# First expert loads and the router's matrix issued beside the output projection, norm and routing in one stage, the first block's rows picked by one-hot products

## The chip, the cores and the metric

The kernel runs on one core of a Trainium2 chip. Its time is the device time of one execution in microseconds (us), and the number compared is the median of several executions. All arithmetic is in 32-bit floating point.

## The reference, cut to what matters

The program is a chain of transformer layers over 512 tokens of width 1024. The last two layers (0 and 1 here) each end in a mixture of experts. The part that the change touches:

```python
h = _rms(x, norm2_w[layer]) * (1 + scale2) + shift2
x = x + gate2 * _hier_moe(h, ...)

def _hier_moe(h, ...):              # 512 tokens, 4 groups of 8 experts
    g_logits = xt @ w_group + b_group
    g_sel = argmax(g_logits)
    e_in = (xt @ w_expert + b_expert)[group g_sel]
    top_v, top_i = lax.top_k(e_in, 2)
    gate = softmax(g_logits)[g_sel] * softmax(top_v)
    # tokens are grouped by expert in blocks of rows; for each block:
    #   (silu(xr @ w1[e]) * (xr @ w3[e])) @ w2[e]
    # and each token's two results are summed with its gates
```

Each expert has 1024x512 matrices w1 and w3 and a 512x1024 matrix w2, so the 32 experts of a layer hold 192 MB (in units of 1024 x 1024 bytes).

## The kernel before

One SBUF tensor (`arena`) is cut into regions by hand, and the eight PSUM banks are used by number. The program is a row of `nc.Block()` stages. In a stage each engine has its own list of instructions, written out by hand with semaphore waits, and all engines meet at a barrier where a stage ends. For each of the two layers the end of the work looks like this:

1. `project_out` (L1742): the mixer's output projection, 64 products, the residual, and the sum of squares for the next norm. The sync engine (SP, which issues the big loads) has only the last two dense weight tiles to issue here (L235).
2. `apply` (L405): a stage of its own. The vector engine (DVE) multiplies x by the reciprocal norm in eight parts (L396), the scalar engine (ACT) adds gain and shift to each (L403) and so makes `h`. SP clears 58 semaphores (layer 0) of stages that have ended.
3. `experts` (L2727), which begins with the routing (`route`, L2486):
   - SP issues the router's matrix `wr` (L2545) and then ten expert loads of 1 MB (L2786), into a ring of 14 slots. A later load n waits until load n-14 has been used.
   - TensorE (PE) multiplies router and `h` (L2551), folds the halves (L2555) and turns `h` into rows of tokens (L2561). ACT copies these rows to SBUF (L2596) and stores them in a DRAM tensor `token_rows` (L2601).
   - DVE picks the experts (L2623 to L2636). PE ranks each token within its expert (L2567, L2568) and counts (L2570). DVE makes one-hot matrices `A` of the ranks for the experts 0 and 1 (L2645), PE makes the token lists of these two experts from them (L2575), and GpSimd (POOL) fetches the rows of the first two blocks from `token_rows` by an indirect DMA (L2833).
   - DVE goes on with the order of the experts by count (to L2661), which SP waits for, and with the place of every token (to L2721). PE lays the places out (`place_tensor`, L2582 and L2587) between block 0 and block 1.
4. The 15 blocks of experts (`KINDS`): a block holds the rows of one ("w"), two ("p") or four ("q") experts. The blocks 0 and 1 (`FIXED`) are always the experts 0 and 1. For block i PE turns the rows of block i+1 (`turn`, L2849), does the first layer in four quarters (`hidden`, L2866), turns the result (L2876), does the second layer (`output`, L2890) and adds the block before into the tokens by a one-hot product (`scattered`, L2904).

Between the blocks 1 and 2 SP waits for more than its ring:

```python
if i == FIXED:
    sp.wait_ge(self.order_ready, 1)
    for n in range(FIXED):
        sp.wait_ge(x_in[n], x_in_before[n] + 16)
```

Before it reads the order it so waits until both early gathers have landed; after that it reads four expert numbers and issues load 10.

Of the kernel before, what the change touches and what calls it, by code (L numbers as in the profile page):

```python
# [45 lines left out]
MOE_SLOT = 2048  # L46
NEG = -30000.0
# [99 lines left out]
class Program:  # L147
    def __init__(self, nc, ins, out):
# [6 lines left out]
        self.output_stored = nc.alloc_semaphore("output_stored")  # L155
        total = 0
# [247 lines left out]

    def apply(self, name, job):  # L405

        nc = self.nc
        scaled, ready = self.sem(name + "_scaled"), self.sem(name + "_ready")
        with nc.Block() as block:
            @block.sync  # L410
            def _(sp):
                self.clear_past(sp)

            @block.vector
            def _(dve):
                self.scale_steps(dve, [job], scaled)

            @block.scalar
            def _(act):
                self.shift_steps(act, [job], scaled, ready)  # L420
        self.release_past()
# [1320 lines left out]
    def project_out(self, name, w0, src, gate, gain, scale, norms=None):  # L1742
# [137 lines left out]
    def even_mixer(self):  # L1880
# [23 lines left out]
        self.project_out("even_out", TILE0["even_out"], o, self.mod["even"][:, 16:24],  # L1904
# [452 lines left out]
    def odd_mixer(self):  # L2357
# [17 lines left out]
        self.project_out("odd_out", TILE0["odd_out"], o, self.mod["odd"][:, 16:24],  # L2375
# [110 lines left out]
    def route(self, layer):  # L2486
# [5 lines left out]
        wr = self.view(self.r0, KD, HALF)  # L2492
# [20 lines left out]
        early_rank, early_own = new(4 * FIXED, 1), new(FIXED, 4)  # L2513
# [17 lines left out]
        s = {n: self.sem("route_" + n) for n in ["w", "lg", "turned", "kept", "stored", "e", "ex", "oh", "rank", "ab", "tok",  # L2531
# [7 lines left out]
        logits, ranks, counts = small[:, 0:144], small[:, 160:288], small[:, 288:320]  # L2539
# [4 lines left out]
        def sync_steps(sp):  # L2544
            sp.dma_start(wr, self.ins["w_route"][layer].rearrange("p (k m) -> p k m", k=KD)).then_inc(s["w"], 16)  # L2545

        def tensor_steps(pe):
            pe.wait_ge(s["w"], 16)
            for k in range(KD):
                part = slice(HALF * (k % 2), HALF * (k % 2) + HALF)  # L2550
                mm = pe.matmul(self.bank[4][part, :], wr[:, k, :], h[:, k, :], start=(k < 2), stop=(k >= KD - 2))  # L2551
# [13 lines left out]
            for b in range(4):  # L2565
                for a in range(b):
# [40 lines left out]
        def vector_steps(dve):  # L2607
            def do(ins):
                self.dve.after(dve, ins)
# [714 lines left out]
```

## Time and profile before

| what | value |
|---|---|
| time, median of 3 runs | 3175.17 us (3168.21 to 3175.97) |
| profiled execution, its own time | 3168.01 us |
| profiled execution, its span | 3166.1 us |
| PE busy | 2819.5 us, 89% of the span |
| DVE busy | 1482.2 us, 47% |
| ACT busy | 644.5 us, 20% |
| data moved by DMA | 615.87 MB |

A share of busy time says how much an engine did, not whether it was waited for. What a change in one place is worth is read from the chain of releases at that place: what an engine waited for, and who ended that wait. The routing of layer 0 stands at about 1682 to 1750 us of the span and the one of layer 1 at about 2583 to 2652 us; both have the same instructions.

### The profile page before, as it was taken

What the parts mean: (1) busy time and instruction counts of PE and PEld (TensorE: products, weight loads), DVE (VectorE), ACT (ScalarE), POOL (GpSimd) and SP (SyncE); (2) the same over time, 40 slices, a digit from 0 to 9 for tenths busy, and PEclk for the clock granted to TensorE, in tenths of its full rate; (3) what the DMA queues carried; (4) which work ended last, traced back from release to release, by engine and by line L of the source; (5) the groups of instructions that cost most, each with busy time, mean ns of one, the idle gap of its engine ahead of it and who ended that gap; (6) DMA issues with size and microseconds to landing.
All of it is one profiled execution on the core that took longest, in us unless ns stands there. A gap on an engine that the chain in (4) does not pass through costs nothing. (4 is left out here: it accounts for less than half of the span.)

```text
span 3166.1 us, 36578 instructions
## 1 busy us (share of the span) xinstructions
PE 2819.5 (89%) x13980; PEld 1796.4 (57%) x13980; DVE 1482.2 (47%) x2937; ACT 644.5 (20%) x1350; POOL 159.7 (5%) x171
## 2 busy tenths in 40 slices
PE   6989779999989998989896989789799878998897
PEld 4877557788838887858653433233387534332242
DVE  4567465657635675456434223132544623232234
ACT  3111455445521110011232000000103421000000
POOL 0000021222100000000100000000000000000000
PEclk8899989999999999999797999899899988999899
DMA  6111147663022222221005999998322028999996
GB/s 242 54 40 61 59 168 258 241 230 118 28 80 80 87 86 73 87 68 67 27 14 228 375 420 385 418 419 342 145 90 71 7 117 336 419 419 383 420 367 250
DMA packets 112200, 615.87 MB, mean 195 GB/s; under 512 B 12864, under 2 KB 13328, under 8 KB 62096
## 3 DMA queue, kind: packets, MB, share of 16 engines
q1 hardware_dynamic: 101456, 576.67, 47.0%
q0 software_dynamic: 9408, 32.54, 2.9%
q10 hardware_dynamic: 1152, 4.19, 0.3%
q8 instruction: 117, 1.92, 0.2%
q14 instruction: 67, 0.55, 0.1%
HBM read 604.84 MB, written 8.51 MB: 194 GB/s over the span
## 5 line engine op out<-in xcount | busy, mean ns | idle before, releaser
L2866 PE MATMUL bank<-arena 128*32 128x512 f32 (+2 forms) x2048 | 440.6, 618 | 35.6 <-DMA arena<-in_w 33.2
L453 PE MATMUL bank<-arena 128*128 128x256 f32 x1776 | 412.1, 386 | 31.5 <-DVE arena L506 11.9
L453 PEld LDWEIGHTS bank<-arena 128*128 128x128 f32 x1776 | 340.6, 193 | 99.1 <-issue 35.6
L2866 PEld LDWEIGHTS bank<-arena 128*32 128x32 f32 (+2 forms) x2048 | 151.4, 137 | 297.1 <-issue 293.9
L2890 PE MATMUL bank<-arena 128*32 128x512 f32 (+2 forms) x1024 | 239.1, 700 | 52.8 <-DMA arena<-in_w 52.8
L2904 PE MATMUL bank<-arena 128*128 128x512 f32 x480 | 237.3, 619 | 8.4 <-DVE arena L3031 4.9
L248 PE MATMUL bank<-arena 128*128 128x512 f32 (+1 forms) x608 | 218.1, 518 | 14.8 <-DVE arena L665 13.9
L2996 DVE SCALAR_TENSOR_TENSOR arena<-bank,arena 128x512 f32<-128x512 f32 x240 | 180.1, 751 | 55.2 <-PE bank L2904 42.5
L2890 PEld LDWEIGHTS bank<-arena 128*32 128x32 f32 (+2 forms) x1024 | 80.2, 148 | 209.0 <-issue 209.0
L248 PEld LDWEIGHTS bank<-arena 128*128 128x128 f32 x608 | 119.7, 198 | 110.4 <-issue 101.5
L2904 PEld LDWEIGHTS bank<-arena 128*128 128x128 f32 x480 | 75.1, 188 | 168.6 <-DVE arena L2996 125.7
L2982 DVE COPY arena<-bank 128x512 f32<-128x512 f32 x30 | 20.8, 692 | 251.4 <-PE bank L2890 251.4
L3006 DVE TENSOR_TENSOR arena<-arena,bank 128x512 f32<-128x512 f32 x30 | 20.6, 688 | 221.4 <-ACT arena L2955 221.4
L1488 PE MATMUL bank<-arena 128*128 128x256 f32 x528 | 118.8, 380 | 0.0
L1124 ACT ACTIVATE arena<-bank 128x256 f32<-128x256 f32 x288 | 93.6, 383 | 87.3 <-PE bank L1044 64.9
L1488 PEld LDWEIGHTS bank<-arena 128*128 128x128 f32 x528 | 100.5, 190 | 14.9
L2935 ACT ACTIVATE arena<-bank 128x512 f32<-128x512 f32 x30 | 18.0, 598 | 438.3 <-PE bank L2849 438.3
L1044 PE MATMUL bank<-arena 128*128 128x128 f32 x576 | 98.7, 294 | 1.5 <-DVE arena L1239 0.8
L1044 PEld LDWEIGHTS bank<-arena 128*128 128x128 f32 x576 | 75.9, 192 | 39.6 <-issue 31.2
L1236 DVE TENSOR_TENSOR arena<-bank,arena 128x256 f32<-128x256 f32 x144 | 61.0, 423 | 75.9 <-PE bank L1029 75.8
L1029 PE MATMUL bank<-arena 128*128 128x128 f32 x576 | 94.3, 286 | 0.6
L2971 DVE COPY arena<-bank 128x512 f32<-128x512 f32 x26 | 18.0, 692 | 159.4 <-PE bank L2849 159.4
(451 smaller groups left out, 4111.0 us busy)
## 6 DMA issues: line engine op xcount, KB each, us to landing
arena<-in_w SPq DMA_DIRECT2D x384, 1024.0 KB, 20.6
arena<-in_dense SPq DMA_DIRECT2D x308, 512.0 KB, 4.5
arena<-core_rows POOLq DMA_DIRECT2D x48, 256.0 KB, 6.4
arena<-in_xT SPq DMA_DIRECT2D x2, 2048.0 KB, 12.6
token_rows<-arena ACTq DMA_DIRECT2D x8, 512.0 KB, 12.6
gdn_gate<-arena POOLq DMA_DIRECT2D x8, 256.0 KB, 2.7
arena<-gdn_gate SPq DMA_DIRECT2D x1, 2048.0 KB, 8.4
arena<-band_bias POOLq DMA_DIRECT2D x2, 1024.0 KB, 6.1
```

The lines of the kernel that those rows point to most:

```text
L248: mm = eng.matmul(dst, w[:, k, :], src[:, k, :], start=(k == 0), stop=(k == KD - 1))
L453: mm = pe.matmul(out, w[:, k, :], x[:, k, :], start=(k == 0), stop=(k == K1 - 1))
L1029: mm = pe.matmul(Y[u][:, q, :], buf[u]["bl"][:, q, :], buf[u]["xl"][:, u, q, :], start=True, stop=True)
L1044: mm = pe.matmul(touched(X[u][:, 2 * q:2 * q + 2, :], l, u), buf[u]["zs"][:, q, :], buf[u]["yn"][:, q, :], start=False, stop=(l == 6), ski ...
L1124: act.activation(gathered(buf[u]["xl"][:, side, :, :], l + 1), touched(X[u], l + 1, side), ACT.Copy).then_inc(kept, 1)
L1236: dve.tensor_tensor(buf[u]["yn"], Y[u][:, 0:2, :], levels[:, l - 1, :, :].to_broadcast([P, 2, P]), ALU.mult).then_inc(s["yn"], 1)
L1488: mm = pe.matmul(product(m, p), s4[:, t, k, :], ht[:, t, k, :], start=(k == 0), stop=(k == K1 - 1))
L2866: mm = pe.matmul(self.bank[2 + t][part, :], xT[i % 2][:, 2 * q + k, part], w[j][:, k, t, :], start=(q == 0 and k == 0), stop=(q == 3 and k ...
L2890: mm = pe.matmul(self.bank[7 - t][part, :], aT[:, 2 * q + k, part], w[j][:, k, 512 * t:512 * t + 512], start=(q == 0 and k == 0), stop=(q ...
L2904: pe.matmul(self.bank[4 + k % 2][:, :], y[i % 2][:, k * P:(k + 1) * P], scatter[i % 2], start=True, stop=True).then_inc(s["summed"], 1)
L2982: dve.tensor_copy(y[i % 2][:, 512:1024], self.bank[6][:, :]).then_inc(s["yk0"], 1)
L2996: dve.scalar_tensor_tensor(self.x[:, k, :], self.bank[4 + k % 2][:, :], gate[:, k:k + 1], self.x[:, k, :], ALU.mult, ALU.add).then_inc(s[" ...
```

## The change

- SP issues the router's matrix and the first 6 (layer 0) or 10 (layer 1) expert loads at the end of its list in `project_out`, into slots that are free by then (`MOE_ORDER`, `MOE_EARLY`).
- The stage `apply` is gone; its steps stand at the head of `experts`, and the router's product k waits for part k of `h` alone.
- The ranks take four products in place of ten, and DVE is released before the counts.
- The rows of block 0 are no longer gathered from DRAM and turned: 32 products of `rows` (tokens x width) with the one-hot `A` of expert 0 write them, turned, into the banks 0 and 1. Only block 1 is gathered.
- `A` now holds the token's own mask too (rank + 1, compared with iota + 1), and is made in one instruction for each expert.
- The token list of expert 1 is made by PE behind the 32 products.
- SP waits for the order alone before load 10. SP's clearing of semaphores stands at the head of `experts`.

```diff
+MOE_ORDER = [[8, 9, 10, 11, 12, 2, 7, 0, 1, 3, 4, 5, 6, 13], list(range(MOE_RING))]
+MOE_EARLY = [6, 10]
...
+    def early_experts(self, sp, layer):
+
+
+        sp.dma_start(self.router(), self.ins["w_route"][layer].rearrange("p (k m) -> p k m", k=KD)).then_inc(self.router_loaded, 16)
+        for n in range(MOE_EARLY[layer]):
+            if n < 4 * FIXED:
+                src = self.ins["w13"][layer, n // 4, :, n % 4 * MOE_SLOT:(n % 4 + 1) * MOE_SLOT]
+            else:
+                src = self.ins["w2"][layer, 0, :, (n - 4 * FIXED) * MOE_SLOT:(n - 4 * FIXED + 1) * MOE_SLOT]
+            sp.dma_start(self.expert_slot(layer, n), src).then_inc(self.expert_loaded[n], 16)
...
             def _(sp):
                 self.load_until(sp, w0 + KD, ahead=0)
+                self.early_experts(sp, layer)
...
         def tensor_steps(pe):
-            pe.wait_ge(s["w"], 16)
+            pe.wait_ge(self.router_loaded, 16 * (layer + 1))
             for k in range(KD):
+                pe.wait_ge(ready, k + 1)
...
             pe.wait_ge(s["oh"], 1)
-            for b in range(4):
-                for a in range(b):
-                    pe.matmul(ranks[:, b * 32:b * 32 + 32], self.C("ones"), oh12[:, a, :], start=(a == 0), stop=False)
-                pe.matmul(ranks[:, b * 32:b * 32 + 32], self.C("stri"), oh12[:, b, :], start=(b == 0), stop=True)
+            pe.matmul(ranks, self.C("stri"), oh12, start=True, stop=False, skip_group_check=True)
+            for a in range(3):
+                mm = pe.matmul(ranks[:, 32 * a + 32:P], self.C("ones"), oh12[:, a:a + 1, :].to_broadcast([P, 3 - a, 32]),
+                               start=False, stop=(a == 2), skip_group_check=True)
+            mm.then_inc(s["rank"], 1)
+            pe.wait_ge(s["kept"], 8)
             for b in range(4):
                 mm = pe.matmul(counts, self.C("ones"), oh12[:, b, :], start=(b == 0), stop=(b == 3))
             mm.then_inc(s["rank"], 1)
             pe.wait_ge(s["early"], 1)
-            for j in range(FIXED):
+            for k in range(KD):
                 for b in range(4):
-                    mm = pe.matmul(early_toks[:, j:j + 1], A[:, 4 * j + b, :], early_own[:, j, b:b + 1],
+                    mm = pe.matmul(self.bank[k // 4][:, k % 4 * P:(k % 4 + 1) * P], rows[:, b, k * P:(k + 1) * P], A[:, b, :],
+                                   start=(b == 0), stop=(b == 3))
+            mm.then_inc(first_turned, 1)
+            pe.wait_ge(s["early"], FIXED)
+            for j in range(1, FIXED):
+                for b in range(4):
+                    mm = pe.matmul(early_toks[:, j:j + 1], A[:, 4 * j + b, :], self.C("tok")[:, b:b + 1],
                                    start=(b == 0), stop=(b == 3))
             mm.then_inc(s["early_made"], 1)
...
-            dve.tensor_copy(early_rank.rearrange("p (e b) o -> p e (b o)", b=4), rk[:, :, 0:FIXED].rearrange("p b e -> p e b"))
-            do(dve.tensor_tensor(early_own, oh12[:, :, 0:FIXED].rearrange("p b e -> p e b"),
-                                 tok.to_broadcast([P, FIXED, 4]), ALU.mult))
-            dve.tensor_tensor(A[:, 0:4 * FIXED, :], c3("iota", 4 * FIXED), wide(early_rank, P), ALU.is_equal
-                              ).then_inc(s["early"], 1)
+
+            do(dve.scalar_tensor_tensor(early_rank.rearrange("p (e b) o -> p e (b o)", b=4), rk[:, :, 0:FIXED].rearrange("p b e -> p e b"),
+                                        1.0, oh12[:, :, 0:FIXED].rearrange("p b e -> p e b"), ALU.add, ALU.mult))
+            for j in range(FIXED):
+                mine = slice(4 * j, 4 * j + 4)
+                dve.scalar_tensor_tensor(A[:, mine, :], c3("iota", 4), 1.0, wide(early_rank[:, mine, :], P), ALU.add, ALU.is_equal
+                                         ).then_inc(s["early"], 1)
+            dve.wait_ge(s["rank"], 2)
             do(dve.tensor_copy(cn, c2))
...
             dve.wait_ge(s["early_made"], 1)
-            dve.tensor_copy(self.early_tok, early_toks).then_inc(s["early_tok"], 1)
+            dve.tensor_copy(self.early_tok[:, 1:FIXED], early_toks[:, 1:FIXED]).then_inc(s["early_tok"], 1)
...
-                route_sync(sp)
+                self.clear_past(sp)
                 for i in range(N + 1):
                     if i == FIXED:
                         sp.wait_ge(self.order_ready, 1)
-                        for n in range(FIXED):
-                            sp.wait_ge(x_in[n], x_in_before[n] + 16)
...
                 pool.wait_ge(self.rows_stored, 64)
                 pool.wait_ge(self.early_ready, 1)
-                for i in range(N):
+                for i in range(1, N):
...
                 route_tensor(pe)
-                turn(0)
...
+                self.shift_steps(act, [job], scaled, ready)
                 route_scalar(act)
                 keep(0)
+                act.wait_ge(self.rows_stored, 64)
...
+                self.scale_steps(dve, [job], scaled)
                 route_vector(dve)
...
-        p.apply(name + "2", (h, p.x, L, p.norm_r[0], p.mod["g1"], mod[:, 24:32]))
-        p.experts(layer, mod[:, 40:48])
+        p.experts(layer, (h, p.x, L, p.norm_r[0], p.mod["g1"], mod[:, 24:32]), mod[:, 40:48])
```

The first place is TensorE's list in layer 0 from the router's product to the first half of block 0. Before, with the ranks at L2567 and L2568, the counts at L2570, the token lists at L2575 and the turn of block 0 at L2849:

```order
L2551 MATMUL bank<-arena 64x512 x8
L2555 MATMUL bank<-arena 128x36 x4
L2561 MATMUL bank<-arena 128x128 x32
L2568 MATMUL bank<-arena 128x32
L2567 MATMUL bank<-arena 128x32
L2568 MATMUL bank<-arena 128x32
L2567 MATMUL bank<-arena 128x32 x2
L2568 MATMUL bank<-arena 128x32
L2567 MATMUL bank<-arena 128x32 x3
L2568 MATMUL bank<-arena 128x32
L2570 MATMUL bank<-arena 128x32 x4
L2575 MATMUL bank<-arena 128x1 x8
```

Behind these stand the 8 turns of L2849 and `hidden`. After, in the same place (L2571 and L2573 are the ranks, L2578 the counts, L2583 the one-hot products, L2589 the token list of expert 1, L2884 is `hidden`):

```order
L2557 MATMUL bank<-arena 64x512 x8
L2561 MATMUL bank<-arena 128x36 x4
L2567 MATMUL bank<-arena 128x128 x32
L2571 MATMUL bank<-arena 128x128
L2573 MATMUL bank<-arena 128x96
L2573 MATMUL bank<-arena 128x64
L2573 MATMUL bank<-arena 128x32
L2578 MATMUL bank<-arena 128x32 x4
L2583 MATMUL bank<-arena 128x128 x32
L2589 MATMUL bank<-arena 128x1 x4
L2884 MATMUL bank<-arena 128x512 x8
```

Ten rank products became four wider ones, and 32 products of 128 columns stand between the counts and the token list, whose own 8 products became 4; the 8 turns behind them are gone.

The second place is SP's list in layer 0, from the last two dense tiles to the wait for the order. L221 is the clearing of semaphores, TENSOR_LOAD the reading of an expert's number. Before:

```order
L235 DMA arena<-in_dense 128x1024 x2
L1746 UNCONDITIONAL_BRANCH
L410 UNCONDITIONAL_BRANCH
L221 ISA x58
L409 UNCONDITIONAL_BRANCH
L2781 UNCONDITIONAL_BRANCH
L2545 DMA arena<-in_w_route 128x512
L2786 DMA arena<-in_w 128x2048 x10
L2799 TENSOR_LOAD arena
```

After:

```order
L240 DMA arena<-in_dense 128x1024 x2
L1740 DMA arena<-in_w_route 128x512
L1746 DMA arena<-in_w 128x2048 x6
L1752 UNCONDITIONAL_BRANCH
L2799 UNCONDITIONAL_BRANCH
L226 ISA x58
L2806 DMA arena<-in_w 128x2048 x4
L2819 TENSOR_LOAD arena
```

The router's matrix and six of the ten loads moved ahead of the stage's end; one barrier (two branches) is gone, and the 58 clears stand ahead of the last four loads.

The third place is DVE's list around the token lists. Before, the wait for PE's token lists is in front of the CAST at L2657:

```order
L2642 COPY arena<-bank 128x8
L2643 TENSOR_TENSOR arena<-arena 128x8
L2645 TENSOR_TENSOR arena<-arena 128x1024
L2647 COPY arena<-bank 128x32
L2653 TENSOR_TENSOR arena<-arena 128x32
L2654 TENSOR_TENSOR arena<-arena 128x1024
L2655 TENSOR_REDUCE arena<-arena 128x32
L2657 CAST arena<-bank 128x2
L2658 TENSOR_TENSOR arena<-arena 128x1024
```

After, with the same wait in front of the CAST at L2673:

```order
L2656 SCALAR_TENSOR_TENSOR arena<-bank,arena 128x8
L2660 SCALAR_TENSOR_TENSOR arena<-arena 128x512 x2
L2663 COPY arena<-bank 128x32
L2669 TENSOR_TENSOR arena<-arena 128x32
L2670 TENSOR_TENSOR arena<-arena 128x1024
L2671 TENSOR_REDUCE arena<-arena 128x32
L2673 CAST arena<-bank 128x1
L2674 TENSOR_TENSOR arena<-arena 128x1024
```

The one-hot matrices come in two instructions of half the size; the place of the CAST in the list is the same, but what it waits for on PE now stands behind the 32 products.

## Rows read from the trace of the kernel before

**Rows 1.** The page: span and TensorE's busy time.
```profile
span 3166.1 us, 36578 instructions
...
PE 2819.5 (89%) x13980; PEld 1796.4 (57%) x13980; DVE 1482.2 (47%) x2937; ACT 644.5 (20%) x1350; POOL 159.7 (5%) x171
```

**Rows 2.** The chain that ended last, layer 1's routing: start, duration, what ran.
```profile
2589.48 2.95 DMA arena<-in_w_route
2592.47 5.45 PE bank L2551 x16
...
2605.77 15.99 DMA token_rows<-arena
...
2629.60 9.11 PE bank L2866 x16
...
2646.46 1.70 PE bank L2582 x16
```

**Rows 3.** Timeline, layer 0: start, duration, engine, line, [idle before, releaser].
```profile
1682.70 5.75 ACT L403 ACTIVATE arena<-arena 128x512 f32<-128x512 f32 x8 [1.02 <-DVE arena L396]
...
1691.48 5.36 PE L2551 MATMUL bank<-arena 128*64 128x512 f32 x16 [11.19 <-DMA arena<-in_w_route]
```

**Rows 4.** Timeline, layer 0: from the ranks to the token lists.
```profile
1705.56 0.41 PE L2568 MATMUL bank<-arena 128*128 128x32 f32 x2 [1.63 <-DVE arena L2635]
...
1707.81 1.18 PE L2570 MATMUL bank<-arena 128*128 128x32 f32 x8
...
1709.31 1.23 DVE L2645 TENSOR_TENSOR arena<-arena 128x1024 f32<-128x1024 f32 x1
...
1710.59 3.57 PE L2575 MATMUL bank<-arena 128*128 128x1 f32 x16 [1.59 <-DVE arena L2645]
```

**Rows 5.** Timeline, layer 0, PE from block 0's turn to the places.
```profile
1725.51 1.97 PE L2849 MATMUL bank<-arena 128*128 128x128 f32 x8 [11.35 <-DMA arena<-token_rows,arena]
1728.70 9.00 PE L2866 MATMUL bank<-arena 128*128 128x512 f32 x16 [1.22 <-ACT arena L2935]
...
1745.30 1.86 PE L2582 MATMUL bank<-arena 128*128 128x31 f32 x16
1747.00 3.82 PE L2587 MATMUL bank<-arena 128*128 128x128 f32 x32
```

**Rows 6.** Timeline, layer 0, DVE: token lists kept, order, last place step; a 128x512 SCALAR_TENSOR_TENSOR.
```profile
1714.27 0.16 DVE L2657 CAST arena<-bank 128x2 uint32<-128x2 f32 x1 [0.90 <-PE bank L2575]
...
1718.11 0.18 DVE L2661 CAST arena<-arena 128x32 int32<-128x32 f32 x1
...
1732.46 0.28 DVE L2721 TENSOR_TENSOR arena<-arena 128x124 f32<-128x124 f32 x1
...
1773.42 0.74 DVE L3027 SCALAR_TENSOR_TENSOR arena<-arena 128x512 f32<-128x512 f32 x1
```

**Rows 7.** SP, layer 0: issues up to 1727, its wait, issues from 1726 on.
```profile
L2786 SPq DMA_DIRECT2D arena<-in_w x10: 424/442/486, 1689.1 to 1693.5; - x10
...
SPq L2806 <- DMA arena<-token_rows,arena: 33.6, 1, 33.6
...
1730.22 27.98 SPq L2786 DMA_DIRECT2D arena<-in_w  x10
```

**Rows 8.** Times to landing: stores of L2601, then gathers of L2833 (min/median/max).
```profile
DMA to landing us min/median/max: 8.1/12.6/16.0
...
DMA to landing us min/median/max: 4.3/8.5/9.7
```

**Rows 9.** Windows: busy time by engine, granted TensorE clock, DMA share, GB/s.
```profile
1705.00:1709.00 4.00, 3.44 (x28) 3.30 (x28) 0.54 (x3) 0.42 (x2) 0.00 (x0) 0.95 1.00 411
1710.00:1714.00 4.00, 3.41 (x16) 3.41 (x16) 3.27 (x5) 0.00 (x0) 0.00 (x0) 0.50 1.00 419
```

**Rows 10.** Waits in layer 0 (1680 to 2240): PE for expert weights.
```profile
PE bank L2890 <- DMA arena<-in_w: 27.7, 9, 6.3
...
PE bank L2866 <- DMA arena<-in_w: 18.4, 5, 7.6
```

More of the change, by code:

```diff
@@ L155, in __init__ @@
         self.output_stored = nc.alloc_semaphore("output_stored")
+        self.expert_loaded = [nc.alloc_semaphore(f"expert_loaded{i}") for i in range(MOE_RING)]
+        self.router_loaded = nc.alloc_semaphore("router_loaded")
         total = 0
@@ L1740, in project_all, with expert_slot, router, project_out @@
         self.release_past()
-    def project_out(self, name, w0, src, gate, gain, scale, norms=None):
+    def expert_slot(self, layer, n):
+        at = self.free0 + 8192 + MOE_SLOT * MOE_ORDER[layer][n % MOE_RING]
+        return self.cols(at, MOE_SLOT)
+    def router(self):
+        return self.view(self.free0 + 4096, KD, HALF)
+    def early_experts(self, sp, layer):
[6 more added lines that the diff above has]
+            sp.dma_start(self.expert_slot(layer, n), src).then_inc(self.expert_loaded[n], 16)
+    def project_out(self, name, layer, w0, src, gate, gain, scale, norms=None):
         nc = self.nc
@@ L2538, in route @@
         small = self.bank[5]
-        logits, ranks, counts = small[:, 0:144], small[:, 160:288], small[:, 288:320]
+        logits, ranks, counts = small[:, 0:144], small[:, 160:288], self.bank[6][:, 0:32]
         toks, early_toks = small[:, 320:320 + BLOCKS], self.bank[4][:, 0:FIXED]
@@ L2723, in vector_steps, with experts @@
             dve.tensor_copy(self.slot_tok, toks).then_inc(s["slots"], 1)
-        return sync_steps, tensor_steps, place_steps, scalar_steps, vector_steps
-    def experts(self, layer, gate):
+        return tensor_steps, place_steps, scalar_steps, vector_steps
+    def experts(self, layer, job, gate):
         nc = self.nc
-        route_sync, route_tensor, place_tensor, route_scalar, route_vector = self.route(layer)
+        route_tensor, place_tensor, route_scalar, route_vector = self.route(layer)
+        scaled, ready = self.sem("moe_norm_scaled"), self.sem("moe_norm_ready")
         f = self.free0
-        ring = self.view(f + 8192, MOE_RING, MOE_SLOT)
         assert f + 8192 + MOE_RING * MOE_SLOT <= self.total - 128
@@ L2765, in experts @@
                                                "yk0", "yk1", "spread", "scatter", "summed", "added"]}
-        loaded = [self.sem(f"moe_slot_loaded{i}") for i in range(MOE_RING)]
+        loads = 6 * NE
+        loaded_before = [layer * ((loads - r + MOE_RING - 1) // MOE_RING) for r in range(MOE_RING)]
         x_in = [self.software_sem(f"moe_rows_gathered{i}") for i in range(2)]
-        x_in_before = [16 * layer * evens, 16 * layer * odds]
-        nth = lambda i: 16 * (i // 2 + 1)
+        x_in_before = [16 * layer * (evens - 1), 16 * layer * odds]
+        nth = lambda i: 16 * ((i + 1) // 2)
         spare_sync, spare_gpsimd, spare_tensor, spare_scalar, spare_vector = self.spare_blocks(layer, gate)
@@ L2776, in slot_in @@
         def slot_in(eng, n):
-            eng.wait_ge(loaded[n % MOE_RING], 16 * (n // MOE_RING + 1))
-            return ring[:, n % MOE_RING, :]
+            r = n % MOE_RING
+            eng.wait_ge(self.expert_loaded[r], 16 * (loaded_before[r] + n // MOE_RING + 1))
+            return self.expert_slot(layer, n)
         with nc.Block() as block:
```

34 lines of the change are left out of this document (11 added, 23 removed).

## The prediction

> **What bounds the kernel now.** I read the page first: TensorE is busy 89% of a span of 3166.1 us [rows 1], but that is an average, and the change touches only two places, the start of the experts in layer 0 and in layer 1. So I read the chain that ended last there. In layer 1 it goes from the load of the router's matrix (2589.48) over the router's product, the turning and ACT's copies to the store of the token rows, which takes 15.99 us to land, then over the gather to the first expert product at 2629.60 and the placing at 2646.46 [rows 2]. TensorE does almost nothing useful for some 37 us of that. Layer 0 is the same story: router's product at 1691.48, placing at 1745.30, a distance of 53.82 us against 53.99 in layer 1 [rows 2, 3, 5]. I therefore work out layer 0 and double it.
>
> After the first blocks PE is in turns bound by itself and by the weights: in layer 0 it waits 27.7 and 18.4 us for weights in 14 waits [rows 10]. So a gain at the front has to be checked against the weight stream too.
>
> **Part 1, apply and experts in one stage.** Before, ACT's last shift ends at 1682.70 + 5.75 = 1688.45. The barrier, the issue and the landing of the router's matrix follow, and the 16 passes of the product, 5.36 us, which end at 1696.84 [rows 3]. After, the matrix is there, and product k follows part k of `h`. ACT's pace is 5.75/8 = 0.72 us a part and PE's mean 5.36/8 = 0.67, so PE keeps up, and one product with its tail is left behind the last part, 1.0 us: end at 1689.4, gain 7.4 us. Bounds: 0.5 us behind (gain 7.9), and PE starting one part late and lagging 2 us behind (gain 6.4). The 58 clears move to SP's list in this stage; behind them stand only loads 6 to 9, which block 1 and block 0's second layer use some 30 us later, and in layer 1 no load: cost nothing. The early loads start when SP's last dense tile is issued; SP has nothing else there, and the output projection has its weights ahead of them in the same queue: nothing as well.
>
> **Part 2, ranks and one-hot.** From the start of the ranks at 1705.56 to the start of the token lists at 1710.59 are 5.03 us [rows 4]. After: four rank products are 8 passes, at the 1.18 us that the 8 passes of L2570 take; one small DVE step and its hand-over, 0.3; a 128x512 SCALAR_TENSOR_TENSOR, 0.74 [rows 6]; hand-over 0.1. Sum 2.3 us, gain 2.7 (bounds 2.2 and 3.0). PE's counts, another 1.18, end at about the same time. DVE's part up to here is not changed. So the one-hot products can start at 1710.59 - 7.4 - 2.7 = 1700.5.
>
> **Part 3, the 32 products.** They are new. Each is two passes, 64 in all. The nearest row is L2587, 32 passes of 128x128 in 3.82 us, 0.12 us each [rows 5]: 7.5 us at the high clock. At 1.2 GHz they would be twice that, 15 us. The granted clock was 0.95 of full while the ranks ran and 0.50 while the token lists ran, behind a short idle time [rows 9]. After the change PE has less idle time ahead of this point, so I take the high clock for most of it, 8.5 us: end at 1709.0. Bounds 7.3 and 15. The Trainium skill (page "TensorE: Matmul & The Clock Gate", "The HAM clock gate") says that the lower clock is the default and that activity has to release it; by that alone the products would begin slow, and this is a rival below. The trace agrees that clock and activity go together here: 0.50 at 1710 after the gap.
>
> Then PE makes expert 1's token list, 8 passes. Before, 16 passes took 3.57 us at the low clock [rows 4], so 0.9 to 1.8; I take 0.9: E = 1709.9. Block 0 needs ACT's copies, 1.2 us behind the products (L2866 was idle 1.22 for them [rows 5]), so `hidden(0)` begins at about 1710.2, where it was 1728.70. That is 18.5 us.
>
> **Part 4, what is late next.** The gain is not all kept. DVE waits at the CAST (L2657) for PE's token list, and that now stands behind the 32 products. From this CAST at 1714.27 to the last place step at 1732.46 + 0.28 are 18.5 us of DVE work [rows 6] that the change leaves alone. Before it was long done when PE reached the placing at 1745.30. After, it ends at E + 18.5 = 1728.4. PE arrives there two half blocks and a turn after `hidden(0)` began: 16.6 us before (1728.70 to 1745.30, the first part at the low clock), so 1726.8 at the latest, and with a warm clock about 1725. It waits 1.6 to 3.4 us. So the placing starts at 1728.4 instead of 1745.30: **gain 16.9 us per layer**, set by DVE and not by the gather.
>
> Other waits in this stretch: block 1's gather is issued at E + 0.5 and lands 4.3 to 9.7 us later [rows 8], needed about 8 us behind E; if it is late by 2 us, the wait at the placing swallows it. The stores of the token rows took up to 16.0 us [rows 8] behind ten queued loads; now at most four loads are ahead, and PE's products give them 10 us more. ACT's new wait for them stands behind `keep(0)`: nothing.
>
> **Part 5, the weight stream.** Before, SP issued ten loads up to 1693.5, idled 33.6 us for the gathers and issued load 10 at 1730.22, some 3 us after its wait [rows 7]. After, it waits for the order alone: that is 4.0 us after the CAST (1718.29 - 1714.27 [rows 6]), plus 3 us of reading: E + 7 = 1716.9. That is 13.3 us earlier than before, 3.6 less than the gain of PE. A load is 1.05 MB at 419 GB/s [rows 9], 2.5 us. Loads 10 to 17 take 20 us, to about 1737.5, and load 18 may start when block 1's first quarter is used, at 1728.4 + 5.4 (places) + 3.4 = 1737.2. From there PE frees a slot every 3.4 us in a one-expert block, so the stream has caught up before the first weight wait. Cost nothing, if this holds.
>
> **Sum.** Two layers by 16.9, and 0.2 for layer 1's longer stretch: 34 us. The profiled execution took 3168.01 us by its own time, 0.2% below the median; it would be 3134. On the median, 3175.17 - 34 = **3141 us**.
>
> **Rivals.**
> *The clock.* The 32 products run at 1.2 GHz to the end: 6.5 us more per layer, all of it in DVE's wait too. Gain 2 x 10.4 = 21: 3154. For it: 0.50 behind the gap [rows 9]. Against it: the products are dense, and the 16 passes of the router's product were not slow to the end.
> *The weight stream decides.* If PE is held by the weights from load 10 on, the gain is that of load 10, 13.3 per layer: 27, 3149. For it: 46 us of weight waits per layer [rows 10]. Against it: ring and one-expert blocks give time to catch up.
> *DVE is no limit.* If PE gets to the placing later than DVE or the products take only 7.3 us and E comes early, the gain is up to 18.5 to 20 per layer: 3136.
> *The other side, block 1's gather behind the weight stream.* Its rows have nothing ahead before; now the loads 10 to 17 are let go 6 us behind it. It decides when it lands over 27 us after its issue, since need (8), slack at the placing (2) and the gain (17) are then used up. If all 14 slots' loads went ahead of its packets, 14 x 2.5 + 4.3 = 39 us, it would cost 12 us more per layer than is won: 3199. Against it: 9.7 us is the longest gather in a trace full of loads [rows 8]. The Trainium skill (page "DMA: Bandwidth & Descriptors", "Issuing engines are not separate DMA queues") says that transfers of all engines share the same 16 DMA engines and interleave, so a gather has no lane of its own. The trace agrees for the stores, 16.0 us with ten loads in flight.
>
> **How the numbers follow.** My forecast (gain of 30 to 38) 0.66, weight stream 0.12, the clock 0.12, DVE no limit 0.06, gather 0.02, and 0.02 that the early gain is lost elsewhere so that nothing is left. Before's own runs lie within 3168 to 3176, so a change under 0.3%, 9.5 us, can't be told from none. The range takes in the clock rival and the gain of 20 per layer with a run at the low end: 3127 to 3156. Faster 0.95, same 0.02, slower 0.03.
>
> **What the profile would show.** Router's product ending about 1 us behind the last shift; the products' start about 12 us behind that shift, and 8 to 9 us for 64 passes; `hidden(0)` 18 us earlier; a new wait of PE for DVE of 1.6 to 3.4 us in front of the placing; load 10 about 7 us behind the CAST; weight waits in sum as before. I am wrong if the products run at the low clock, if weight waits grow by what was won, or if PE waits for the gather in front of block 1's turn.

## The result, and the profile after

The changed kernel takes 3149.72 us (median of 4 runs, 3144.84 to 3150.47), the kernel before, run beside it, 3175.57 us (4 runs, 3168.21 to 3177.84). The ratio is 0.9926, with a 95% interval of 0.9913 to 0.9939: 19 to 28 us faster. The forecast was 3141 us, a gain of 34. So the sign and the place are right, and about 8 of the 34 us are missing.

The page of the changed kernel (its profiled run took 3149.28 us), against [rows 1]:

```profile
span 3147.5 us, 36685 instructions
...
PE 2838.1 (90%) x14052; PEld 1818.0 (58%) x14052; DVE 1483.0 (47%) x2937; ACT 644.1 (20%) x1350; POOL 158.2 (5%) x169
```

The span is 18.6 us shorter, and TensorE is busy 18.6 us longer. Its 72 additional instructions account for part of that; the other part are old products that take longer, as the timeline shows.

Because one trace reaches layer 0's routing a few us earlier or later than another (1680 to 1685 us in the traces of this study), I count from an anchor: DVE's first step of the norm's scaling, at 1681.97 in the trace of before and at 1684.23 in that of after. A "+" in the text is a time from there, in layer 0 unless it says otherwise. Timeline of TensorE after the change: start, duration, engine, line, [idle before, releaser].

```profile
1685.92 6.15 PE L2557 MATMUL bank<-arena 128*64 128x512 f32 x16 [3.37 <-ACT arena L408]
...
1700.79 0.80 PE L2571 MATMUL bank<-arena 128*128 128x128 f32 x2 [1.64 <-DVE arena L2649]
1701.38 1.33 PE L2573 MATMUL bank<-arena 128*128 128x96 f32 x6
1702.52 1.90 PE L2578 MATMUL bank<-arena 128*128 128x32 f32 x8
1704.22 8.91 PE L2583 MATMUL bank<-arena 128*128 128x128 f32 x64
1712.97 0.95 PE L2589 MATMUL bank<-arena 128*128 128x1 f32 x8
1714.36 7.12 PE L2884 MATMUL bank<-arena 128*128 128x512 f32 x16 [0.43 <-issue]
1721.32 1.03 PE L2867 MATMUL bank<-arena 128*128 128x128 f32 x8
1722.19 7.05 PE L2884 MATMUL bank<-arena 128*128 128x512 f32 x16
1732.60 3.59 PE L2596 MATMUL bank<-arena 128*128 128x31 f32 x16 [3.37 <-DVE arena L2737]
1736.01 6.46 PE L2601 MATMUL bank<-arena 128*128 128x128 f32 x32
1742.31 7.05 PE L2884 MATMUL bank<-arena 128*128 128x512 f32 x16
```

The first experts' product (L2884, L2866 before) starts at +30.13 instead of +46.73. The placing (L2596 and L2601, before L2582 and L2587 of [rows 5]) starts at +48.37 instead of +63.33, behind a wait of 3.37 us for DVE. But it then takes 9.71 us to the start of block 1's product, where it took 5.35 us before. So block 1 starts at +58.08 instead of +68.68: of 16.6 us at block 0, 15.0 are left at the placing and 10.6 behind it. Layer 1 does the same: idle 3.37 us, L2596 3.59, L2601 6.56, block 1's product at +58.58. The distance between the two layers' anchors shrank by 10.5 us (900.77 to 890.26), which says that what is gained at block 1 arrives whole at the next layer.

The windows of the changed kernel over this stretch say why the placing got slower: busy time of each engine, then the granted TensorE clock as a share of full, DMA share, GB/s.

```profile
1726.00:1730.00 4.00, 3.23 (x8) 1.14 (x6) 3.59 (x14) 0.60 (x1) 0.00 (x0) 1.00 1.01 426
1730.00:1734.00 4.00, 1.40 (x7) 1.43 (x7) 2.35 (x5) 0.00 (x0) 0.00 (x0) 0.67 1.01 424
1734.00:1738.00 4.00, 4.00 (x20) 4.00 (x20) 0.79 (x2) 0.00 (x0) 1.00 (x2) 0.50 1.02 418
1738.00:1742.00 4.00, 4.00 (x23) 4.00 (x22) 0.00 (x0) 1.68 (x3) 0.92 (x1) 0.55 1.00 413
1742.00:1746.00 4.00, 4.00 (x14) 2.02 (x13) 0.00 (x0) 0.71 (x2) 0.00 (x0) 1.00 0.70 281
```

The clock was at 1.00 until the wait, fell in it, and stayed at about half (1.2 GHz; the windows give 0.50 and 0.55) for the whole placing. DVE's list shows whom PE waited for, against [rows 6]:

```profile
1714.03 0.16 DVE L2673 CAST arena<-bank 128x1 uint32<-128x1 f32 x1 [6.65 <-PE bank L2589]
1717.87 0.18 DVE L2677 CAST arena<-arena 128x32 int32<-128x32 f32 x1
...
1732.18 0.28 DVE L2737 TENSOR_TENSOR arena<-arena 128x124 f32<-128x124 f32 x1
```

DVE stands still for 6.65 us in front of a 0.16 us CAST, because the token list that it copies is now made behind the 32 one-hot products.

### The profile page after: what moved, and what is told of

Read it like the earlier page. It is cut to its first block and busy times, and to the rows that moved or that the text cites. A ratio compares the mean times of both kernels' runs of the same rounds, so it can differ in the third digit from the quotient of the medians.

```text
span 3147.5 us, 36685 instructions
## 1 busy us (share of the span) xinstructions
PE 2838.1 (90%) x14052; PEld 1818.0 (58%) x14052; DVE 1483.0 (47%) x2937; ACT 644.1 (20%) x1350; POOL 158.2 (5%) x169
## 5 line engine op out<-in xcount | busy, mean ns | idle before, releaser
L2884 PE MATMUL bank<-arena 128*32 128x512 f32 (+2 forms) x2048 | 437.2, 619 | 30.9 <-DMA arena<-in_w 30.1
L2884 PEld LDWEIGHTS bank<-arena 128*32 128x32 f32 (+2 forms) x2048 | 149.9, 137 | 289.6 <-issue 288.6
```

The source lines that it names most:

```text
L2884: mm = pe.matmul(self.bank[2 + t][part, :], xT[i % 2][:, 2 * q + k, part], w[j][:, k, t, :], start=(q == 0 and k == 0), stop=(q == 3 and k ...
```

## The experiments

The theory after the result: DVE's 6.65 us make PE wait 3.37 us at the placing, and that wait costs twice, as idle time and as 4.4 us of placing at the low clock. The rivals: the gather of block 1 or the weight stream limits what is won; the one-hot products are a bad exchange whoever waits; the early loads carry the gain, or none of it. Nine of the ten kernels below change one or two things in the changed kernel or put parts of it back, and one repeats it. Ratios are against the kernel before, with the 95% interval.

**1. The CAST later.** DVE's wait for the token list and its CAST stand 5.9 us of DVE's own work later, behind the order (L2677) and eight small steps, where it still waits 0.70 us for the list and no longer 6.65:

```diff
-            dve.wait_ge(s["early_made"], 1)
-            dve.tensor_copy(self.early_tok[:, 1:FIXED], early_toks[:, 1:FIXED]).then_inc(s["early_tok"], 1)
...
             x1, x2 = (x.rearrange("p a b -> p (a b)") for x in (m1, m2))
+            dve.wait_ge(s["early_made"], 1)
+            dve.tensor_copy(self.early_tok[:, 1:FIXED], early_toks[:, 1:FIXED]).then_inc(s["early_tok"], 1)
```

> DVE keeps the token list of expert 1 (the CAST of L2673) 5.9 us of its own work later, just behind the ranks of both choices (L2688), and so no longer stands still while PE makes the 32 one-hot products. Theory A (what was lost of the forecast is PE's wait for DVE in front of the placing, 3.37 us, and the low clock that follows it, which stretches the 16 + 32 passes of the placing from 5.35 to 9.71 us): DVE's last place step ends some 5.9 us earlier, PE does not wait, the placing takes about 5.4 us, block 1 starts 7.7 us earlier in each layer: 15 us less than the changed kernel, about 3135. Theory B (the weight stream decides from load 10 on): PE starts block 1 earlier but waits that much more for weights; within 3 us of the changed kernel.

Measured: 3138.85 us, ratio 0.9902 (0.9887 to 0.9918). Better than the change, but not the 3135 that was expected. The timeline of this kernel:

```profile
1711.09 7.12 PE L2885 MATMUL bank<-arena 128*128 128x512 f32 x16 [0.43 <-issue]
1721.17 1.95 PE L2868 MATMUL bank<-arena 128*128 128x128 f32 x8 [2.96 <-DMA arena<-token_rows,arena]
1722.91 7.91 PE L2885 MATMUL bank<-arena 128*128 128x512 f32 x16
1730.66 1.86 PE L2596 MATMUL bank<-arena 128*128 128x31 f32 x16
1732.37 3.82 PE L2601 MATMUL bank<-arena 128*128 128x128 f32 x32
1736.02 7.05 PE L2885 MATMUL bank<-arena 128*128 128x512 f32 x16
```

The wait for DVE is gone and the placing is as fast as before, 1.86 and 3.82 us. In its place PE now waits 2.96 us for block 1's gather, one piece earlier, and pays behind that wait too (a turn of 1.95 instead of 1.03, a half block of 7.91 instead of 7.05). Block 1's product starts at +55.05. In layer 1 it is the same: a wait of 2.73 us, and +55.06. SP's timeline of this kernel from 1706 to 1730, and then the gather's own line, with its start and its time to landing:

```profile
1710.73 17.15 SPq L2807 DMA_DIRECT2D arena<-in_w  x7
```

```profile
L2852 POOL DMA_INDIRECT arena<-token_rows,arena x1: 1035/1035/1035, 1711.8 to 1711.8; - x1
...
DMA to landing us min/median/max: 9.4/9.4/9.4
```

The order is ready sooner, so SP issues load 10 at 1710.73, 1.1 us ahead of the gather. The gather takes 9.4 us. In the changed kernel SP issues load 10 at 1720.69, 5.7 us behind the gather, whose line reads:

```profile
L2851 POOL DMA_INDIRECT arena<-token_rows,arena x1: 1194/1194/1194, 1715.0 to 1715.0; - x1
...
DMA to landing us min/median/max: 4.6/4.6/4.6
```

It lands in 4.6 us, half the time. In layer 1 the two times are 9.2 and 4.8 us.

**2. The wait filled.** The changed kernel with PE kept busy where it waits for DVE. The four products write to a bank that nobody reads:

```diff
                         pe.wait_ge(s["kept0"], 2)
+                        for _ in range(4):
+                            pe.matmul(self.bank[7][:, :], self.C("ones"), self.x[:, 0, :], start=True, stop=True)
                         place_tensor(pe)
```

> The changed kernel with four more products of 128x512 (8 passes, about 3.4 us) on PE in front of the placing, whose result nothing reads: PE works where it waited for DVE. The moment at which DVE is ready is not moved. Theory A says that the 4.4 us by which the placing became longer come from the clock that falls in the wait: with PE busy the placing takes about 5.4 us instead of 9.7 and the kernel is 8 to 9 us faster than the changed one, though it does more work. Rival: the placing is slower for another reason (DMA traffic beside it, what it reads), then it stays at 9.7 us and the time is the same or a little above.

Measured: 3136.38 us, ratio 0.9894 (0.9879 to 0.9909). The timeline of this kernel, and behind it one of its windows:

```profile
1722.24 7.05 PE L2884 MATMUL bank<-arena 128*128 128x512 f32 x16
1729.13 3.60 PE L2936 MATMUL bank<-arena 128*128 128x512 f32 x8
1732.56 1.95 PE L2596 MATMUL bank<-arena 128*128 128x31 f32 x16
1734.34 3.82 PE L2601 MATMUL bank<-arena 128*128 128x128 f32 x32
1737.99 7.05 PE L2884 MATMUL bank<-arena 128*128 128x512 f32 x16
```

```profile
1734.00:1738.00 4.00, 4.00 (x38) 4.00 (x38) 0.79 (x2) 1.79 (x3) 1.91 (x2) 1.00 1.02 424
```

DVE's last place step ends where it did (+48.20), and so the placing starts where it did (+48.28), but PE is busy until then, and the placing takes 5.4 us instead of 9.7; the clock is 1.00. Block 1's product is at +53.71, 4.37 us before the changed kernel (4.42 in layer 1). DVE, and the DMA traffic beside the placing (424 GB/s against 418), are as before. Four products without any use make the kernel 0.3% faster, some 11 us where 8 to 9 were expected. That the clock is a cost of its own, apart from the wait, is shown by this.

**3. No one-hot products.** Both first blocks are gathered and turned as before; one stage, early loads, four rank products remain.

```diff
-            for k in range(KD):
-                for b in range(4):
-                    mm = pe.matmul(self.bank[k // 4][:, k % 4 * P:(k % 4 + 1) * P], rows[:, b, k * P:(k + 1) * P], A[:, b, :],
-                                   start=(b == 0), stop=(b == 3))
...
-            for j in range(1, FIXED):
+            for j in range(FIXED):
...
                 route_tensor(pe)
+                turn(0)
```

> One part undone: the rows of block 0 are gathered from DRAM and turned as before, both token lists are made as in one step, the 32 one-hot products are gone; the early loads, the merged stage and the four rank products stay. Theory A': the one-hot products stand in DVE's way, and what they replace had become cheap once no weight loads are queued ahead of the stores (they land in 2.8 to 3.9 us). Then: token lists done about 7 us earlier, gather lands about 5 us behind, hidden of block 0 starts within 2 us of the changed kernel, DVE is ready before PE, the placing is warm: block 1 starts 5 us earlier per layer, about 3140, faster than the changed kernel by 10. Rival (the products are what brought the gain, the gather is slow): hidden of block 0 starts 8 us or more later, 3160 or more.

Measured: 3142.6 us, ratio 0.9914 (0.99 to 0.9927), and its timeline:

```profile
1701.22 3.57 PE L2583 MATMUL bank<-arena 128*128 128x1 f32 x16
1710.33 1.97 PE L2861 MATMUL bank<-arena 128*128 128x128 f32 x8 [5.53 <-DMA arena<-token_rows,arena]
1713.52 9.35 PE L2878 MATMUL bank<-arena 128*128 128x512 f32 x16 [1.22 <-ACT arena L2947]
```

Block 0 starts at +32.34, only 2.2 us behind the changed kernel. Its first half takes 9.35 us instead of 7.12, but PE never waits for DVE, and block 1's product is at +54.64 (+55.06 in layer 1): 3.4 us *before* the changed kernel, where 5 were expected. So in the change as built the one-hot products, its most laborious part, lose 3.4 us per layer. In the medians this is inside the intervals, so it rests on the timelines of both layers.

**4. The same with the gap filled.** `no_onehot`, and four such products without use behind the token lists, where PE waits 5.53 us for the gather:

```diff
                 route_tensor(pe)
+                for _ in range(4):
+                    pe.matmul(self.bank[7][:, :], self.C("ones"), self.x[:, 0, :], start=True, stop=True)
                 turn(0)
```

> This is the version without the one-hot products (both first blocks are gathered and turned, no_onehot), with four 128x512 products by ones into a free bank put behind the token lists, where TensorE was idle for 5.53 us until the gather of block 0 had landed. It asks how much of what the one-hot products can give (block 1's products at +50.2 in late_cast_wait against +54.64 in no_onehot, from the norm's first step) is earlier rows, and how much is that TensorE comes warm to block 0. Warmth theory: the turn takes 1.03 us instead of 1.97 and the first half block 7.1 instead of 9.35, all at the same gather time (turn at about +29.2), so block 1 begins at +51.5, 3.1 us per layer before no_onehot, and the time is about 3136. Rival, the rows' time alone counts: the turn and the half block stay at 1.97 and 9.35 us although the gap is filled, block 1 stays at +54.6 and the time at about 3143. If the four products take more than the gap, because they begin at the low clock, up to 1.7 us of the gain is lost.

Measured: 3138.39 us (3131.02 to 3144.62), ratio 0.9892 (0.9869 to 0.9914), timeline:

```profile
1705.50 5.22 PE L2921 MATMUL bank<-arena 128*128 128x512 f32 x8
1711.16 1.09 PE L2861 MATMUL bank<-arena 128*128 128x128 f32 x8 [0.45 <-DMA arena<-token_rows,arena]
1713.48 7.12 PE L2878 MATMUL bank<-arena 128*128 128x512 f32 x16 [1.22 <-ACT arena L2949]
```

The rows land at the same time (the turn starts at +29.16 against +29.15), but the turn takes 1.09 instead of 1.97 us and the half block 7.12 instead of 9.35. Block 1's product is at +51.55 (+52.64 in layer 1, where the gather landed later and the turn starts at +30.25). The granted clock is 1.00 at 1709 to 1713, where it was 0.50 in `no_onehot`. So a TensorE that comes to block 0 at the full clock is a large part of what the one-hot products can give: of the 4.5 (layer 0) and 4.6 us (layer 1) by which `late_cast_wait` (9 below) starts block 1 ahead of `no_onehot`, the filled gap gives 3.1 and 2.4. The intervals of `no_onehot` and this kernel overlap, so this too rests on the timelines.

**5. The early expert loads taken away.** `MOE_EARLY = [0, 0]`; the router's matrix is still early.

> One part undone: no expert load is issued beside the output projection, all ten stand behind the 58 clears in the merged stage; the router's matrix is still early. Theory: block 0 needs its first four loads 26 us behind the stage's start, they take 10, so they are not late; the stores of the token rows have up to ten loads ahead and take up to 16 us again, so that the gather of block 1 is issued about 2 us later and lands at the limit of its need; what that costs is hidden in the wait in front of the placing. Same as the changed kernel within 3 us. Rival: the early loads are what brought the gain; then 8 us or more slower than the changed kernel.

Measured: 3143.33 us, ratio 0.9917 (0.9903 to 0.9931). Not slower than the change. The stores of the token rows landed late again. The view lists the eight stores of both layers, but has times to landing only for the four of layer 1:

```profile
L2615 ACTq DMA_DIRECT2D token_rows<-arena x8: 325/326/353, 1692.0 to 2583.8; - x8
...
DMA to landing us min/median/max: 9.9/13.2/16.5
```

In the changed kernel the same view gives 2.8/3.8/3.9, again for layer 1 alone. For layer 0 there is a wait instead: here POOL waits for the stores until 1712.79, 16.3 us behind the issue of the last one, and in the changed kernel it does not wait for them at all. But block 0 needs no stored rows now, and block 1 has DVE's wait to cover its late gather: PE waits 1.41 us for the gather and then only 1.71 us for DVE, where it was 3.37 us in one piece. Block 1's product is at +55.44 in layer 0 and +58.36 in layer 1, where PE waits 3.35 us for DVE in one piece again.

**6. Only the early issues.** The norm's stage is put back, the one-hot products taken out. What remains: early loads and router's matrix, four rank products, SP's shorter wait.

```diff
+        p.apply(name + "2", (h, p.x, L, p.norm_r[0], p.mod["g1"], mod[:, 24:32]))
...
-                self.shift_steps(act, [job], scaled, ready)
                 route_scalar(act)
...
-                self.scale_steps(dve, [job], scaled)
                 route_vector(dve)
```

> What is left of the change when the one-hot products are undone and the norm's apply is again a stage of its own: the early loads and router's matrix, the four rank products, the short wait of SP. By the profile before: the router's product starts 2.5 us earlier (no load to wait for), ranks and lists take 3.5 us less, the stores of the token rows no longer take 16 us, the gather lands behind the token lists in 5 us. Block 1 starts at about 59 us instead of 68.7: 9.5 us per layer, 19 in all, 3154 against a median before of 3173. If early loads are worth nothing by themselves (the kernel without them was as fast as the changed one) because something else hides them, it is worth 6 us or less in all.

Measured: 3151.88 us, ratio 0.9938 (0.9924 to 0.9951). The router's product starts at +6.78 (before +9.51), the ranks at +20.50 (+23.59), block 0's turn at +32.62 (+43.54), block 1's product at +58.09 and, in layer 1, +58.69. This gives 10.6 us in layer 0 at the same point where the whole change gives 10.6. The largest piece is the stores: their time to landing is 2.6/4.0/5.9 us (least, median, most; 5.3 to 5.9 in layer 0, where four loads are still issued 8 us ahead of them, 2.6 to 2.7 in layer 1, where none is) and not 8.1/12.6/16.0 [rows 8]. In layer 0 the first gather so waits for the token list alone and goes out at +27.86 instead of +38.98.

**7. The change again**, beside the same runs of before as the kernels 6, 8 and 9.

> The changed kernel once more, unchanged, as the measure for the others on the same chip. Its ratio to the kernel before should be 0.992 to 0.993 again; block 1 starts 58.1 us behind the first vector step of the norm's apply, in both layers within 0.5.

Measured: 3147.88 us (3142.33 to 3151.4), ratio 0.9924 (0.9911 to 0.9938). Block 1 starts at +58.11 in layer 0 and at +58.73 in layer 1, a little outside the 0.5 us.

**8. SP's wait for the gather put back**, alone:

```diff
                         sp.wait_ge(self.order_ready, 1)
+                        sp.wait_ge(x_in[1], x_in_before[1] + 16)
```

> The changed kernel with SP's wait for block 1's gather put back in front of load 10, nothing else. The gather is issued 1 us behind the CAST and lands 4.6 us later, some 2 us behind the order's end, so load 10 goes out about 1.5 to 2 us later. Theory: the stream catches up before its first wait, and the time is that of the changed kernel within 2 us. Rival (the weight stream decides): 3 to 4 us more.

Measured: 3146.14 us, ratio 0.9917 (0.9904 to 0.9931), block 1's product at +58.06, though load 10 goes out 1.5 us later (+38.00 against +36.46): no difference that can be told from the change.

**9. Both: the CAST later and SP's wait.** The two diffs of 1 and 8 together, so that nothing is issued ahead of the gather.

> The late CAST, and SP waits again for block 1's gather before load 10. With the late CAST alone the gather took 9.4 us (4.6 in the changed kernel), since loads 10 to 13 were let go 1 us ahead of it, and PE waited 2.7 to 3.0 us for it with the clock falling. Theory A (DVE's wait and the clock set the changed kernel's loss; the gather then takes over): gather lands in 4.6 us, PE waits for nothing between block 0 and the placing, block 1 starts 50.3 us behind the first vector step instead of 55.1 (late CAST alone) and 58.1 (changed): 15 us less than the changed kernel, 9 less than the late CAST alone. Theory B (weight stream): load 10 now goes out 7 us later than with the late CAST alone, PE pays it back in weight waits and the time is that of the late CAST alone.

Measured: 3128.41 us (3124.22 to 3129.4), ratio 0.9861 (0.9846 to 0.9876). This is the fastest version, 44 us faster than before and 19 us faster than the change in the same comparison. Its timeline:

```profile
1713.38 7.12 PE L2886 MATMUL bank<-arena 128*128 128x512 f32 x16 [0.43 <-issue]
1720.34 1.03 PE L2869 MATMUL bank<-arena 128*128 128x128 f32 x8
1721.21 7.05 PE L2886 MATMUL bank<-arena 128*128 128x512 f32 x16
1728.10 1.86 PE L2596 MATMUL bank<-arena 128*128 128x31 f32 x16
1729.80 3.82 PE L2601 MATMUL bank<-arena 128*128 128x128 f32 x32
1733.45 7.04 PE L2886 MATMUL bank<-arena 128*128 128x512 f32 x16
```

From block 0 to block 1 PE waits for nobody, and every piece has its fast duration. Block 1's product is at +50.19 (+50.47 in layer 1), 18.5 us before that of the old kernel. Load 10 goes out at +38.01, 8.2 us later than in `late_cast`, and yet PE's waits for expert weights in layer 0 are 25.3 and 16.8 us, not more than before.

**10. The fastest version without early expert loads.**

> This is the fastest version so far (late_cast_wait: DVE's wait for the token list behind the order, SP waits for block 1's gather) with the router's matrix and the expert loads not issued early, MOE_EARLY = [0, 0] (the matrix itself stays early). In the change as built the early expert loads were worth nothing, since the token rows are not needed by block 0 and DVE's wait covered the rest. Theory: here no wait covers them. The token rows land 13 to 16.5 us after their issue instead of 3.8, so block 1's gather is issued some 1 to 2 us later than in late_cast_wait and takes 6.6 us as in no_early; TensorE waits about 1.4 us for it in layer 0 and more in layer 1, so block 1 begins at +51.6 or later instead of +50.2, and the time is 3131 to 3135. Rival: the early loads are worth nothing here either, block 1 at +50.2 and a time of 3128.

Measured: 3133.57 us, ratio 0.9875 (0.9859 to 0.9892). In layer 0 PE waits 0.79 us for the gather and block 1's product is at +51.83; in layer 1 there is no wait (+50.63). The expectation had a longer wait in layer 1, and that did not come. By the timelines the early loads are worth 1.6 and 0.2 us here at most: 0.6 of the 1.6 is already there at block 0's start (+30.75 against +30.12), where the changed kernel's own two traces give +30.13 to +30.64. The medians differ by 5 us, with overlapping intervals.

## Why the prediction was right and where it was wrong

*Part 1* (one stage) said that the router's product ends 1.0 us behind the last shift, gain 7.4 us. It ends 1.36 us behind it (1685.92 + 6.15 against ACT's last shift, which ends at +6.48), and the gain is 7.0 us. Right, within its bounds of 6.4 and 7.9.

*Part 2* (ranks) said 2.3 us from the ranks to the one-hot products, gain 2.7 (2.2 to 3.0). It took 3.43 us, gain 1.6, outside the bounds. It priced ranks and counts at the old rows' 1.18 us each and said that the counts "end at about the same time" as DVE's one-hot step. In the run the clock was at 0.51 here: the ranks took 1.7 us, and the counts (L2578), which stand ahead of the products in PE's list, took 1.90 and were the last to end. In `early_only`, where TensorE had the full clock here, the same ranks and counts took 0.92 and 1.06 us.

*Part 3* (32 products) said 8.5 us; they took 8.91 us (8.75 to the next instruction). Right, as was the choice between the bounds: the first ones run at half clock, then at full. (Its reason, less idle time ahead of them, was not: at their start the clock was at half, where before it was at 0.95 for the ranks [rows 9].) The clock rival is refuted for this place. The Trainium skill's rule (page "TensorE: Matmul & The Clock Gate", "The HAM clock gate"), that activity has to release the faster clock, agrees with the windows of the trace after: 0.51 at 1700.5 to 1704.5, in the ranks and counts, 0.57 at 1704 to 1708 and 1.00 at 1708 to 1712, in the products.

Together the token list ended 1.8 us later than forecast, at +29.69 instead of +27.93, and `hidden(0)` was won by 16.6 us and not 18.5.

*Part 4* is the step that failed. Its mechanism was right: DVE, held by the CAST, is late next, and PE waits for it; forecast 1.6 to 3.4 us, measured 3.37. DVE's 18.5 us behind the CAST were 18.4. But it took this wait at its idle length and the placing behind it at its old 5.35 us. In the run the granted clock fell in the wait, and the placing took 9.71 us: 4.4 us more per layer, 8.7 in both. I had weighed the clock where TensorE comes out of an idle time (Part 3) and not where my own sum put a new one. The 16.9 us per layer therefore split into: 1.9 us lost up to the placing, 4.4 lost in it, 10.6 left. At block 1 `pe_fill` gives these 4.4 back (4.37) and nothing else.

The 0.2 us that the sum adds for layer 1 came of two views read together: the timeline has layer 1's placing at 2646.30, and its distance is 53.83 us, the same as in layer 0.

Two such layers give 21 us. The medians give 24 to 26, and the interval 19 to 28; the remaining 3 to 5 us are not assigned, and can be the spread between runs.

*Part 5* (weight stream) was right that it costs nothing: PE's waits for weights in layer 0 are 28.7 and 15.4 us against 27.7 and 18.4 [rows 10]. Load 10 was issued at 1720.69, 6.8 us behind the end of the token list (forecast 7). The measured 3149.72 is all but the 3149 of the rival that had the weight stream decide. That is chance: in `pe_fill` block 1 starts 4.4 us earlier while the order, and so load 10, stays where it was, and in `late_cast_wait` load 10 goes out 1.5 us later than in the changed kernel and block 1 starts 7.9 us earlier. Both kernels are faster by that gain and more, so the stream did not hold PE.

*The other side*, the gather behind the weight stream, was a real mechanism of the wrong size. It did not act in the changed kernel, where the next loads go out 5.7 us behind the gather, which takes 4.6 us. It acted in `late_cast`, where loads go 1 us ahead: 9.4 us, and block 1 4.9 us later than in `late_cast_wait`. The Trainium skill (page "DMA: Bandwidth & Descriptors", "Issuing engines are not separate DMA queues") says that transfers of all engines share the same DMA engines; these two numbers agree with it. The 27 us at which it would have decided were never near.

What the parts of the change are worth, from block 1's product in layer 0: early issues, shorter ranks and SP's shorter wait 10.6 us; one stage 3.4; the one-hot products minus 3.4 as built, and plus 4.5 when DVE does not wait for them and the gather goes ahead of the loads. Of these 4.5, 3.1 are to be had by a filled gap alone (`gather_fill`; 2.4 of 4.6 in layer 1). The signs depend on the order in which parts are added: the early expert loads alone were not run, and beside the one-hot products they give 1.6 us or less.

Not tried, though it is the obvious other cure: the token list ahead of the one-hot products on TensorE. DVE's wait for the list is also all that keeps it from rewriting `A` (L2734) before the products have read it, so that order would need a wait of its own there; what it would give is open. Open is why the times of `pe_fill` and `late_cast_wait` are some 2 to 4 us better than twice their gain at block 1; in both, the distance between the two layers' anchors also shrank by 2 to 2.5 us more than that gain, so it lies in layer 0 behind block 1's start.

## What to carry to other kernels

When a sum puts a new wait in front of a row of small products, price two things: the idle time, and the products behind it at the half clock. Here 3.4 us of waiting cost 7.7. When an engine's result is moved back, look for everything that stands behind it in *another* engine's list for no reason: a 0.16 us copy, moved past a few instructions that need nothing from it, raised the gain from 24 to 33 us, and to 44 with the gather ahead of the loads. And where a small urgent transfer and a stream of 1 MB loads are released by one event, issue the small one first.

## What the runs showed of the hardware

- An idle time of 3.37 us behind 15 us of dense products is followed by 9.7 us at a granted clock of 0.50 to 0.55; one of 1.71 us in `no_early` still by a window of 0.57, with the second part of the placing at 5.44 us instead of 3.82. The 1.41 us wait in the same kernel was followed by a turn of 1.09 and a half block of 7.05 us, so no loss.
- The length of an idle time does not decide this alone. In front of the ranks stand 1.63 us of it before and 1.64 after the change; behind it the ranks run at a granted clock of 1.00 (1705.5 to 1707.8) before and of 0.50 (1700.8 to 1702.5) after. What made the difference was not tried.
- TensorE that is busy does not always have the full clock: between 1700.5 and 1704.5 of the changed kernel it was busy for 3.71 of 4.00 us with products of 32 to 128 columns, at 0.51.
- Products without use, put into a wait, saved 4.4 us in each layer (`pe_fill`) and 3.1 and 2.4 us in the two layers (`gather_fill`).
- Stores of 512 KB landed in 2.8 to 3.9 us where all ten loads of 1 MB had been issued in the stage before (layer 1 of the changed kernel), in 5.3 to 5.9 us with four loads issued 8 us ahead (layer 0 of `early_only`), and in up to 16.5 us with ten (layer 1 of `no_early`). An indirect gather landed in 4.6 us with the next load issued 5.7 us behind it, and in 9.4 us with one issued 1 us ahead.
